# First attention of a two-block kernel: values computed straight into channel rows, by pairs of heads, with other banks and another order of the weight splits

## The reference, cut to what matters

```python
s = jnp.einsum("bhqd,bhqjkd->bhqjk", qc, kg).astype(jnp.float32) * scale
s = jnp.where(mask, s, -jnp.inf)
pr = jax.nn.softmax(s.reshape(b, H, MOBA_QCHUNK, -1), axis=-1).reshape(s.shape)
return jnp.einsum("bhqjk,bhqjkd->bhqd", pr.astype(vg.dtype), vg)
...
y_att = moba_attention(q, k, v).reshape(b, L, ATT_INNER) @ w_attn_out
merged = jax.nn.sigmoid(g_ssd) * y_ssd + jax.nn.sigmoid(g_att) * y_att
return merged @ w_out
```

## Time and profile before

| what | us |
|---|---|
| median of 3 runs | 797.02 |
| lowest, highest | 796.76, 798.28 |
| profiled execution, its own time | 796.26 |
| its span | 794.5 |
| PE busy / DVE busy / ACT busy | 738.9 / 465.0 / 321.6 |
| of the chain that ended last: PE / DVE / DMA / ACT | 64% / 14% / 13% / 6% |

### The profile page before, as it was taken

One profiled execution on the slowest core, in us unless ns is written; L12 is line 12 of the kernel. 1 busy time (PEld: TensorE's weight loads), 2 busy tenths in 40 slices (PEclk: granted clock), 3 DMA queues, 4 the chain that ended last, 5 costly groups with the idle time before them and its releaser, 6 DMA issues.

```text
span 794.5 us, 11035 instructions
## 1 busy us (share of the span) xinstructions
PE 738.9 (93%) x4636; PEld 557.4 (70%) x4636; DVE 465.0 (59%) x825; ACT 321.6 (40%) x479; POOL 17.9 (2%) x15
## 2 busy tenths in 40 slices
PE   7999999999999999996799798779999999999998
PEld 7978886888877886563345254337999966678886
DVE  6878965455766665531333221128777698875673
ACT  6464446536437225210111110127674634255631
POOL 0000000000000000000000000001100003000000
PEclk9999999999999999998879988899999999999999
DMA  9765542333439849899999999997453654433311
GB/s 314 238 206 185 163 158 104 106 107 106 139 110 410 294 189 422 315 366 420 419 421 417 421 421 421 419 398 268 148 197 120 214 184 160 156 109 106 106 53 54
DMA packets 63153, 189.97 MB, mean 239 GB/s; under 512 B 7481, under 2 KB 11835, under 8 KB 51132
## 3 DMA queue, kind: packets, MB, share of 16 engines
q1 hardware_dynamic: 61326, 184.44, 62.7%
q10 hardware_dynamic: 1774, 4.79, 1.8%
HBM read 188.16 MB, written 1.05 MB: 238 GB/s over the span
## 4 chain that ended last, share of the span: by engine, by line
PE 64%; DVE 14%; DMA 13%; ACT 6%; issue 2%; POOL 1%; SPq 0%; DVEq 0%; POOLq 0%
PE pb L519 60%; DMA raw<-in_w_exp_up 6%; DMA WHo<-in_w_exp_up 4%; DVE rawo L1785 4%; PE pb L528 4%; ACT WH L1282 2%; DMA WHo<-in_w_exp_down 1%; DVE cv_ L1893 1%; ACT arena L1441 1%; DVE arena L2054 1%; DMA X<-in_x 1%; POOL small L2690 1%; DVE arena L2100 0%; ACT arena L1476 0%; ACT arena L1310 0%
## 5 line engine op out<-in xcount | busy, mean ns | idle before, releaser
L1785 DVE TENSOR_TENSOR rawo<-raw,WH 128x2048 fp32r<-128x2048 f32 (+5 forms) x80 | 172.7, 2175 | 64.5 <-ACT WH L1282 64.4
L519 PE MATMUL pb<-WH,HTh 128*128 128x512 f32 (+2 forms) x384 | 155.0, 404 | 3.9 <-DVE rawo L1785 1.7
L1282 ACT ACTIVATE WH<-raw 128x2048 fp32r<-128x2048 f32 (+5 forms) x80 | 144.0, 1822 | 21.1 <-PE pb L519 15.1
L519 PE MATMUL pb<-rawo,HTh 128*128 128x512 f32 (+2 forms) x384 | 147.7, 385 | 0.0
L519 PE MATMUL pb<-WH,HTl 128*128 128x512 f32 (+2 forms) x384 | 147.5, 384 | 0.0
L519 PEld LDWEIGHTS pb<-WH,HTh 128*128 128x128 f32 x384 | 72.3, 188 | 22.5 <-issue 5.1
L519 PEld LDWEIGHTS pb<-rawo,HTh 128*128 128x128 f32 x384 | 72.2, 188 | 14.3
L519 PEld LDWEIGHTS pb<-WH,HTl 128*128 128x128 f32 x384 | 72.4, 188 | 13.0 <-issue 1.0
L519 PE MATMUL pb<-WH,arenao 128*128 128x512 f32 x192 | 59.7, 392 | 1.2 <-DVE arenao L1819 1.2
L519 PE MATMUL pb<-raw,arena 128*32 128x256 f32 (+1 forms) x256 | 49.7, 491 | 10.8 <-DMA raw<-in_w_exp_up 6.3
L519 PE MATMUL pb<-arena 128*32 128x256 f32 (+6 forms) x252 | 58.1, 429 | 1.6 <-ACT arena L1698 0.7
(11 more groups left out here) (363 smaller groups left out, 1266.2 us busy)
## 6 DMA issues: line engine op xcount, KB each, us to landing
raw<-in_w_in SPq DMA_DIRECT2D x46, 1024.0 KB, 5.1
raw<-in_w_exp_up SPq DMA_DIRECT2D x18, 1024.0 KB, 21.1
arena<-in_w_exp_gate SPq DMA_DIRECT2D x13, 1024.0 KB, 22.4
arena<-in_w_exp_down SPq DMA_DIRECT2D x12, 1024.0 KB, 15.8
WHo<-in_w_exp_down SPq DMA_DIRECT2D x9, 1024.0 KB, 23.5
raw<-in_w_out SPq DMA_DIRECT2D x8, 1024.0 KB, 5.2
raw<-in_w_exp_gate SPq DMA_DIRECT2D x8, 1024.0 KB, 16.0
WHo<-in_w_exp_up SPq DMA_DIRECT2D x8, 1024.0 KB, 21.4
```

The costliest lines, as they stand in the source:

```text
L519: return e.matmul(o, l, r, start=start, stop=stop, skip_group_check=True)
L1282: e.activation(h_, r_, ACT.Copy).then_inc(hi.sem, hi.mark(k))
L1785: e.tensor_tensor(l_, r_, h_.bitcast(F32), ALU.subtract).then_inc(lo.sem, lo.mark(k))
```

## The change

- **Values.** For a pair of heads V (128 keys x 64 channels) is now stationary, and the transposed weights stream: 2 matmuls of 256 columns and 2 of 128. The two heads go to the lower and upper 64 partitions of one bank, bank 4, for each of the 8 pairs. The result already stands by channels.
- **Division.** DVE divides the weights before they are turned: `shares(p)`, one reciprocal and 4 scalings of 128 or 256 columns in place. PE's `weights_T` waits for it instead of for ACT's exponential. `divided` is gone.
- **Split of the output.** ACT's `output_high(p)` and DVE's `output_low(p)` (128 x 256 each) split each pair as it comes. `attended_T` with its 16 transposes and the `high` and `low` behind it are gone. Bank 4 is free for pair p+1 once `output_low(p)` is done.
- **Order on DVE.** Scores of pair j, `shares(j-1)`, `output_low(j-4)`, the copy of the even head, then both chunks' splits at the end of the step.
- **Banks.** The filling takes (6, 7), (5, 6), (7, 5) in turn until the rounds are over, and the rounds have banks 0 to 4 instead of 0 to 5.
- **Places in memory.** OT's high part lies where Q was. The fetch of one expert tile (i = 3), which overlaps it, waits for `wao` instead of `yn` and is issued with tiles 5 and 6. `wao`'s rows are read in another grouping.

```diff
-        for key, w, rows_ in (("wao", wao, "(p c)"), ("wso", wso, "(p c)"), ("wo", wo, "(c p)")):
+        for key, w, rows_ in (("wao", wao, "(c p)"), ("wso", wso, "(p c)"), ("wo", wo, "(c p)")):
...
             ring.of = range(4)
-            held_o = []
+            fill_at.clear()
+            fill_at.extend(((6, 7), (5, 6), (7, 5)))
...
             def weights_T(h):
                 o = ring.take(("p", h), (ve, ac)[h % 2])
-                ac.wait_ge(e, ("e", h))
+                ve.wait_ge(e, ("sn", h // 2))
...
-            def values(h):
-                hc, pv = (h % 8) * 64, P1[:, h % 4, 0:384]
-                if hc == 0:
-                    held_o[:] = [ring.take(("o", h // 8, t), ve, at=4 + t) for t in range(2)]
-                (ve, ac)[h % 2].wait_ge(e, ("p", h))
+            def values(p):
+                o = ring.take(("o1", p), ve, at=4)
+                for h in (2 * p, 2 * p + 1):
+                    (ve, ac)[h % 2].wait_ge(e, ("p", h))
                 ve.wait_ge(e, (("v", 1), 0))
                 ac.wait_ge(e, (("v", 1), 1))
-                mul(held_o[0][:, hc:hc + 64], pv[:, 0:128], V[:, 0, h * 64:h * 64 + 64])
-                mul(held_o[1][:, hc:hc + 64], pv[:, 128:256], V[:, 0, h * 64:h * 64 + 64], True, False)
-                mul(held_o[1][:, hc:hc + 64], pv[:, 256:384], V[:, 1, h * 64:h * 64 + 64], False, True).then_inc(
-                    mm.sem, mm.mark(("pv1", h)))
+                for keys, q in ((0, 0), (1, 128)):
+                    for i in range(2):
+                        h = 2 * p + i
+                        pv = P1[:, h % 4, 0:384]
+                        ins = mul(o[64 * i:64 * i + 64, q:256], V[:, keys, h * 64:h * 64 + 64],
+                                  pv[:, 256 * keys:256 + 128 * keys], keys == 0, keys == 1)
+                ins.then_inc(mm.sem, mm.mark(("pv1", p)))
...
-            ring.of, ring.i = range(6), 0
+            ring.of, ring.i = range(5), 0
...
-                if k in (1, 2):
-                    attended_T((4 * k - 4, 4 * k - 2))
...
# scalar
+            def output_high(p):
+                mm.wait_ge(e, ("pv1", p))
+                e.activation(OT[0][:, p, :], pb(("o1", p))[:, 0:256], ACT.Copy).then_inc(ac.sem, ac.mark(("oTh", p)))
+
             for j in range(11):
+                if j >= 4:
+                    output_high(j - 4)
...
# vector
+            def shares(p):
+                ac.wait_ge(e, ("e", 2 * p + 1))
+                e.reciprocal(rsum[:, :, 2 * p:2 * p + 2], ssum[:, :, 2 * p:2 * p + 2]).then_inc(ve.sem, ve.mark(("rs", p)))
+                ve.wait_ge(e, ("rs", p))
+                for h in (2 * p, 2 * p + 1):
+                    for t, cut in enumerate((slice(0, 128), slice(128, 384))):
+                        sv = S1[h % 8][:, cut]
+                        ins = e.tensor_scalar(sv, sv, rsum[:, t, h:h + 1], None, ALU.mult)
+                ins.then_inc(ve.sem, ve.mark(("sn", p)))
+
+            def output_low(p):
+                ac.wait_ge(e, ("oTh", p))
+                e.tensor_tensor(OT[1][:, p, :], pb(("o1", p))[:, 0:256], OT[0][:, p, :].bitcast(F32),
+                                ALU.subtract).then_inc(ve.sem, ve.mark(("oT", p), ("o1", p)))
 
             for j in range(11):
                 if j < 8:
                     scores(2 * j)
                     scores(2 * j + 1)
-                if j == 7:
-                    divided(7)
-                fill(1)
+                if 1 <= j <= 8:
+                    shares(j - 1)
+                if j >= 4:
+                    output_low(j - 4)
                 if 2 <= j <= 9:
                     h = 2 * j - 4
                     if h >= 4:
-                        mm.wait_ge(e, ("pv1", h - 4))
+                        mm.wait_ge(e, ("pv1", (h - 4) // 2))
                     drain_t(("p", h), P1[:, h % 4, 0:384])
-                fill(1)
-                if j == 10:
-                    divided(15)
+                fill(2)
+            output_low(7)
...
# sync
-            early = {used_before(("wso", 0), 4): (0, 1, 2), used_before(("wso", 1), 4): (3, 4),
-                     used_before(("wo", 0), 4): (5, 6)}
+            early = {used_before(("wso", 0), 4): (0, 1, 2), used_before(("wso", 1), 4): (4,),
+                     used_before(("wo", 0), 4): (3, 5, 6)}
```

More of the change, by code:

```diff
@@ L271, in program @@
         GS, GA = area(8704, 2), area(10752, 2)
-        XD, XE, Y, O, MG = XN, sg_, K, Q, XS
+        XD, XE, Y, MG = XN, sg_, K, XS
         conv = cv_[:, :].rearrange("p (j l) -> p j l", j=4)
@@ L279, in program @@
         OT, MT = (tuple(arena_r[:, o:o + 2048].rearrange("p (c l) -> p c l", c=8) for o in (hi_at, 0))
-                  for hi_at in (6656, 2048))
+                  for hi_at in (2560, 2048))
         hb = lambda a: a.unsqueeze(2).to_broadcast([128, 16, 64])
@@ L545, in gemm @@
                     gemm_chunk(name, key, c, o, lhs, ready)
-            open_fill, fill_at = {}, deque([6])
+            open_fill, fill_at = {}, deque([(6, 7)])
             def fill(n):
@@ L552, in fill @@
                     if c == 0:
-                        open_fill[name] = [ring.take((name, t), drainer, at=fill_at[0] + t) for t in range(2)]
-                        fill_at.rotate(1)
+                        open_fill[name] = [ring.take((name, t), drainer, at=fill_at[0][t]) for t in range(2)]
+                        fill_at.rotate(-1)
                     gemm_chunk(name, key, c, open_fill[name], lhs, ready, turned)
@@ L730, in tensor @@
                 if j >= 3:
-                    values(2 * j - 6)
-                    values(2 * j - 5)
+                    values(j - 3)
             def decay_rows(t, h0):
@@ L740, in decay_rows @@
                 ins.then_inc(mm.sem, mm.mark(("lm", t, h0)))
-            def attended_T(js):
-                for j in js:
-                    o = ring.take(("oT", "T", j), ve)
-                    ve.wait_ge(e, ("o", 1, 0), ("o", 1, 1))
-                    for c in (j, j + 1):
-                        for t in range(2):
-                            o_ = (c - j) * 256 + t * 128
-                            ins = turn(o[:, o_:o_ + 128], O[:, t, slice(c, c + 127 * 8 + 1, 8)])
-                    ins.then_inc(mm.sem, mm.mark(("oT", "T", j)))
             def states(t, g):
@@ L788, in tensor @@
             ring.of = range(8)
+            fill_at.clear()
+            fill_at.append((6, 7))
             gemm(("wao", 0), ("wao", 0), OT, "oT", (ve, ve))
@@ L1154, in tensor @@
             ring.of, ring.i = range(4), 0
-            fill_at.append(4)
+            fill_at.append((4, 5))
             for o_ in range(2):
@@ L1189, in tensor @@
             fill_at.clear()
-            fill_at.append(6)
+            fill_at.append((6, 7))
             held_o2 = [ring.take(("o2", t), ve, at=4 + t) for t in range(2)]
@@ L1467, in scalar @@
                     e.activation(Z, Z, ACT.Silu).then_inc(ac.sem, ac.mark("z"))
-                if k in (1, 2):
-                    high("oT", OT, 4 * k, after=("pv1", 15), first=4 * k - 4)
                 if k:
@@ L2019, in scores @@
                 ins.then_inc(ve.sem, ve.mark(("s", h), ("mx", h)))
-            def divided(h):
-                ac.wait_ge(e, ("e", h))
-                for t in range(2):
-                    rs, ss_ = rsum[:, t, h - 7:h + 1], ssum[:, t, h - 7:h + 1]
-                    e.reciprocal(rs, ss_).then_inc(ve.sem, ve.mark(("rs", h, t)))
-                    mm.wait_ge(e, ("pv1", h))
-                    ve.wait_ge(e, ("rs", h, t))
-                    e.tensor_tensor(hd(O[:, t, (h - 7) * 64:(h + 1) * 64]), hd(pb(("o", h // 8, t))[:, :]),
-                                    rs.unsqueeze(2).to_broadcast([128, 8, 64]), ALU.mult).then_inc(
-                        ve.sem, ve.mark(("o", h // 8, t)))
+            def shares(p):
[11 more added lines that the diff above has]
+                                ALU.subtract).then_inc(ve.sem, ve.mark(("oT", p), ("o1", p)))
             for j in range(11):
@@ L2091, in vector @@
                     skipped(k // 2, k % 2)
-                if k in (1, 2):
-                    low("oT", OT, 4 * k, first=4 * k - 4)
                 if k:
```

7 lines of the change are left out of this document (3 added, 4 removed).

## The result

| | before | after |
|---|---|---|
| median, us | 796.95 (796.14 to 798.28, 5 runs) | 801.49 (798.71 to 804.08, 5 runs) |
| ratio, 95% interval | | 1.0057 [1.0035, 1.0079] |
| the profiled execution, us | 796.26 | 801.49 |
| its span, us | 794.5 | 799.7 |

A second measurement of the same kernel gave 1.0063 [1.0041, 1.0085]. The forecast was 798.0, with a range from 795.0 to 800.3. The times of after also lie further apart than those of before: 5.4 us against 2.1.

The account below looks back on a forecast made before the run. PE was taken to bound the kernel up to 234 us, DMA the experts from about 343. Terms of +1.2, -1.74, -1.1, +0.4 and +0.9 gave -0.3 us; with one clock drop the forecast was 798.0, range 795.0 to 800.3.

Parts of the forecast that it names:

- values, a pair: PE's attention loop: a pair's values take 0.96 us instead of 1.37, saving 0.41; bounds 0.66 and 1.42.
- wait at values(1): Attention loop: PE waits 3.5 us for DVE's `output_low` to free bank 4, and is 2.1 late.
- wait at values(5): Attention loop: the chain repeats and PE waits about 2.4 us for bank 4; the loop ends 1.2 later.
- last round's product against before, clock held: End of the rounds: loop +1.2, transposes gone -1.74, bank waits gone -1.1, waiting for DVE's mask +0.4 us.
- `wao`'s bank: Behind the rounds: `wao` waits 0.6 us for a bank ACT drains, costing nothing because `yn` is not ready anyway.
- fetch and rows: DMA: the moved fetch of one 1 MB expert tile and the other grouping of `wao`'s rows cost nothing.
- `cq`'s bank: Second block, near 563 us: PE waits 0.9 us for ACT's sigmoid to drain the bank, or 0 if a bubble swallows it.
- the sum with the clock held: Whole kernel: all terms without a clock drop sum to -0.3 us, 796.7; as a rival it had chance 0.20.
- the clock: Behind the new waits in the attention loop: one drop to 1.2 GHz, up to +1.6 us, +1.3 in all; chance 0.42.
- its start moves with PE: Experts' stage: bound by DMA from about 343 us on, only its start shifts with PE; no change beyond the shift.
- two drops: Rival, attention loop: the second new wait also loses the clock, another 1.6 us, 799.8 in all; chance 0.13.
- No overlap: Rival, values: the two heads run one after the other, 1.42 us a pair, nothing saved, 800.0 with one drop; chance 0.10.

Follow-up runs that it names:

- all dummies: The changed kernel with useless matmuls keeping PE busy in three waits, at values(1), values(5) and ahead of the last round's product: ratio 0.9993, median 796.51 us.
- before with dummies: The kernel before with 3 useless matmuls in PE's wait of 0.77 us ahead of the last round's product: ratio 0.9994.
- the ring at 18: The changed kernel with the ring of banks set to 18 behind the rounds, so every later product lies in the bank it had before: ratio 1.0050.
- the dummies at values(1) and values(5): The changed kernel with 12 useless matmuls on PE ahead of values(1) and 7 ahead of values(5), the waits kept: ratio 1.0005.
- the splits between: The changed kernel with DVE's fillings and weight splits again on both sides of the copy, as before the change: ratio 1.0082.

## Why the prediction was wrong, point by point

| step | forecast | measured |
|---|---|---|
| values, a pair | 0.96 (0.66 to 1.42) | 0.80 |
| DVE: scores, shares, `output_low` | 1.11, 1.15, 0.35 | 1.11, 1.13, 0.42 |
| wait at values(1) | 3.5 | 3.49 |
| wait at values(5) | 2.4 | 2.30 |
| last round's product against before, clock held | -1.2 | -1.5 (all dummies; start-up of 0.9 taken off) |
| `wao`'s bank | 0.6, hidden | 0.73, hidden |
| fetch and rows | 0 | 0 |
| `cq`'s bank | +0.9 | +1.1 |
| experts' stage | 0 (shifted) | +1.7, +2.3 (two profiles of after), +0.6 (all dummies) |
| the sum with the clock held | -0.3 | -0.6 (0.9993); -0.1 against before with dummies |
| the clock | +1.3, one drop | +5.6 by dummies; 3.1 and 4.6 in the spells of two profiles |

**The failed step is the clock.** Nearly everything that I worked out from rows of durations came within 0.4 us of what was measured, except the experts (below), and the kernel in which PE is kept busy in the three waits shows about the sum. That the sum fits is partly luck: in its profile the last round's product is 0.3 better than forecast, `cq` 0.2 and the experts 0.6 worse. A further wait, 0.41 us at values(4), was not forecast. Two figures of the prediction are off by 0.1, and nothing hangs on them: from 145.9 to 143.87 it is 2.0 and not 2.1, and 796.7 less 1.2 is 795.5. The step that failed reads: "So I count one drop to 1.2 GHz ... +1.3 in all" (this is +1.6 for the drop and -0.3 for the rest; in the forecast of 798.0 the drop stands with 1.3). Three things in it were wrong.

First, the place. I looked for drops at the two new waits only. The wait ahead of the last round's product stood in the forecast as one that gives back 0.4 us, so it was seen to grow, from 0.77 to 1.28; what a longer idle time does to the clock was not asked there. In ten profiles with a wait of 1.28 to 1.40 us at this place seven have a spell behind it; in seven with dummies in it (one of them before with its shorter wait), none.

Second, the size. I took 1.65 us for a drop, from the earlier trace rows. Spells come in 3.4 and in 6.8 us: 1.7 or 3.4 us of PE. At the last round five of the seven are the longer kind.

Third, the length was taken for the measure. "With 1.54 us idle (243 to 248) it stays at 1.00" is right for its place: twelve profiles have this wait ahead of yn's transposes (L528), and none has a spell behind it.

```profile
246.74 2.04 PE L528 MATMUL pb<-c,XN 128*128 128x128 f32 x16 [1.54 <-DVE XN L2117]
```

Nor has any of the nine profiles with a wait of 1.31 to 1.51 us near 136, nor any of the four waits of 1.25 at values(1) and values(5) in the two kernels with `output_low` first and one bank. The shorter wait ahead of the last round has one in seven of ten. The wait of 3.49 (2.92 in one kernel) had a spell in five profiles of five, that of 2.30 in one of five. So a row without a drop holds for its own place and not for another of the same length. What sets the places apart, no run tests.

**A second step failed: "its start moves with PE".** The experts' stage was put at a pure shift. In the two profiles of after it is 1.7 and 2.3 us longer than before. The prediction named such a change as a sign of being wrong; the cause stays open.

The wide spread of the times of before and after was in reach of the prediction, too: 1.5 us between three runs is about what a spell of 3.4 costs.

Of the rivals, "two drops", 799.8, was the nearest; it had a chance of 0.13 and was still 1.7 low. "No overlap" is excluded by 0.80 a pair, where the prediction's estimate for one head after the other was 1.42. The Trainium skill, TensorEngine Tiling (Array Packing), Theoretical Speedup, gives two column tiles up to twice the speed; 1.42 to 0.80 is a factor of 1.8, within that.

**What stays open.** The stretch from the experts' fetch to the transposes behind the experts is 210.4 to 211.0 us in all eight profiles of kernels built on before, and 211.2 to 215.1 in all twelve of those built on the changed kernel (212.7 and 213.2 in after). That the stage would only be shifted was an assumption of the prediction, and it is false by 0.2 to 4 us. It is not the fetch, not the rows of `wao`, and not the rotation of the banks (212.9 with the ring at 18). The longest, 215.1, belongs to a kernel that reaches the stage early; but after reaches it late. Of the 4 us that the dummies at values(1) and values(5) gave, the profiles show 2.9, and 1.4 of that lies in this stage.

## What to carry to other kernels

A new wait on an engine whose clock depends on its being busy has two prices: its own length and, with some chance in each execution, a spell at half clock behind it, here 1.7 or 3.4 us for a wait of 0.8 to 3.5. The chance depends on the place as well as on the length: here none in twelve for 1.54 us at one place, seven in ten for 1.3 to 1.4 at another. So cost every wait that a change makes longer, also one that is already there and is said to give time back; and where the wait can't go, let the engine compute something useless into a bank that is free or that it is about to overwrite. And when an output buffer goes from many to one, put its drain first in the draining engine's step: moving that one instruction was worth 6.5 us here, a second bank 8, both with what they spared of the clock.

## What the runs showed of the hardware

- A wait of 0.77 us in a PE that is otherwise busy from 220 to 235 us can be followed by 6.8 us at 1.2 GHz. The Trainium skill, TensorE: Matmul & The Clock Gate, A second HAM failure mode, tells of a kernel whose short idle times between groups, while it cycles through banks, make the clock fall and rise; the traces here agree as to the kind, with waits that come once and not in each step.
- A spell can begin ahead of the wait's end: in the kernel with the splits between, the granted clock in 143 to 148 is 0.79, which puts the fall at about 145.9, while PE goes on at 146.73. In two more of the five profiles with the long wait at values(1) it begins 0.3 us ahead of the wait's end.
- 12 matmuls of 128x512 whose result is never read held the clock and cost nothing, since PE had nothing else to do.
- Two heads side by side in the array's columns, with 64 stationary columns each, took 0.80 us for 2 x 256 and 2 x 128 moving columns, less than the scores with the same columns in two row halves (0.86).
